# Column sums of the norms: folded on DVE and summed by one full product, in place of products with 32 columns of ones and a picking product

## Chip, cores and metric

One core of a Trainium2 chip runs the whole program. The metric is the device time of an execution in microseconds. TensorE is PE in the profile (PEld its weight loads), VectorE is DVE, ScalarE is ACT, GpSimd is POOL.

## What is computed

A sequence of 256 tokens with 1024 channels goes through two transformer stacks. The first has two layers (a state space branch and windowed attention, then a gated feed-forward part), the second four layers, each with another mixer (a conformer convolution, a gated linear recurrence, an mLSTM, stick-breaking attention) and a gated feed-forward part with a convolution. Everything is float32. What the change touches are the norms after each branch:

```python
def rms_norm(x, w):
    y = xf * lax.rsqrt(jnp.mean(xf * xf, axis=-1, keepdims=True) + NORM_EPS)
    return y * w
...
def layer_norm(x, g, b):
    mu = jnp.mean(xf, axis=-1, keepdims=True)
    var = jnp.mean(jnp.square(xf - mu), axis=-1, keepdims=True)
    y = (xf - mu) * lax.rsqrt(var + LN_EPS)
    return y * g + b
...
x = x + mixed @ w_out[i]                                  # first stack, then rms_norm
...
x = layer_norm(DN_ALPHA * x + (1.0 + gate1) * y, ...)     # second stack
```

## The kernel before, in words

The residual `x` lies in SBUF as 8 tiles of 128 channels (partitions) by 256 tokens. `h` is its normalised copy, the input of the next projections; `t1` (`sb_t` in the trace) holds squares. `L` are four PSUM banks for products of weights (`job_bank`), `M` four for the rest (`mix_bank`).

A **job** is a projection to two tiles of output channels. `run` computes one with products of 128x128 weights and 256 columns (L892). Weights come through a ring of five slots of 1 MB, filled by the SP queue (L664), in the order of use.

At the end of a branch (`w_out`, `w_down` and so on) four jobs give the 8 tiles of `x`. Around the norm the program is cut in halves of 128 tokens, so that the norm of one half runs beside products of the other. The last `ns` jobs (1 or 2) are computed as **half passes** (`half_pass`, L947): first tokens 0 to 127 of them, then tokens 128 to 255 into the banks M[2] and M[3]. Then `heads` computes the first two jobs of the next stage, first half of both (with the h of tokens 0 to 127), and then the second half. A half of a job is 16 products where the contraction has 8 tiles, 32 where it has 16 and 44 where it has 22. `hooks` puts other instructions behind the n-th product of a half pass.

A norm needs for each token the sum over 1024 channels of x squared, and in the "mean" norms (second stack) of x as well. The order of the work around it:

- For each job that is done in full, DVE updates x (`add_to_x` L2488, `gated_to_x` L2338) and ACT writes the squares of the two tiles to `t1` (`square_pair`, L1771). In the "mean" norms DVE adds up squares into t1[0:2] and values into t1[2:4] (`gather`, L2354 and L2356); in the "square" norms it makes one add, t1[0:2] += t1[4:6] (L2306).
- `pair_sums` (L980, last=True): four products of 32 columns of ones with t1[0..3], 256 tokens each, into the four row groups of M[0]. It stands behind the first half pass of the first tail job.
- For each half the tail job's tiles are updated (`add_tail` L2498, `gated_tail` L2378), squared by ACT, and summed by `tail_sums` with `group_sums` (L961): products with 32 columns of ones, in "square" one for each tile of squares, in "mean" also one for each tile of x.
- DVE copies M[0] to SBUF (`keep_parts`, L2300), and `whole_sums` adds the four groups and spreads the total over 128 partitions by a product with a picking matrix (`pick`): one in "square" (L1007), two in "mean" (L1001, L1002), into M[1].
- ACT takes the root (L1791, L1818), DVE the reciprocal (L2291, L2413), and DVE (L2294) or DVE and ACT (L2405, L2408, L1804) make h.

The first half's group stands in the second half pass of the tail (behind 8 products), the second half's in the first half pass of the heads (behind 8, or 12 with ns = 2), each with the picking products 2 ("mean") or 4 ("square") further on (`join_hooks`).

There are 11 such norms: four "square" with ns = 1 in the first stack; in the second stack four "mean" with ns = 1 (after the feed-forward parts of layers 0 to 2 and after the mLSTM) and three with ns = 2 (after `pw2` of the conformer, the recurrence and the stick-breaking attention). The last norm of the second stack (`final_norm`) and the norm within the conformer go their own ways, though the latter shares `whole_sums`, `keep_parts` and `centre_half`. In the feed-forward parts of the first stack and of layers 0 and 1 of the second, work for the conditioning of later layers goes along; there two transposes (L1102) stand between the tail's second half pass and the heads. Behind pw2 the order is written out by hand:

```python
half_pass(pw2[2], h_tile, 0).then_inc(s.half_done, 1)
half_pass(pw2[0], h_tile, 1, h_first)
half_pass(pw2[1], h_tile, 1)
pair_sums("mean")
half_pass(pw2[3], h_tile, 0).then_inc(s.half_done, 1)
pair_sums("mean", True)
half_pass(pw2[2], h_tile, 1, bank=M[2], hooks=join_hooks("mean", pw2, 2, 0))
```

So DVE gets jobs 0 and 1 of pw2 in full only just ahead of the tail, where the other norms get them earlier.

Of the kernel before, what the change touches and what calls it, by code (L numbers as in the profile page):

```python
# [366 lines left out]
def build(nc, a, out):  # L367
    with ExitStack() as ctx:
# [494 lines left out]
        def _(pe):  # L863
# [94 lines left out]
            def group_sums(norm, ks, c):  # L958

                def into(g, src):  # L960
                    return pe.matmul(M[0][32 * g:32 * g + 32, c], ones[:, 0:32], src, start=False, stop=True,  # L961
                                     skip_group_check=True)
                if norm == "mean":
                    for k in ks[::2]:
                        into(0, x[:, k, c])
                        into(1, x[:, k + 1, c])
                        into(2, t1[:, k, c])
                        mm = into(3, t1[:, k + 1, c])
                else:
                    for k in ks:  # L970
                        mm = into(k % 4, t1[:, k, c])
                return mm

            def pair_sums(norm, last=False):

                due(s.sq_ready)
                if last:
                    pe.wait_ge(s.acc_ready, due(s.acc_ready))
                    for g, k in enumerate((2, 3, 0, 1) if norm == "mean" else range(4)):
                        pe.matmul(M[0][32 * g:32 * g + 32, 0:T], ones[:, 0:32], t1[:, k, :], start=True, stop=True,  # L980
                                  skip_group_check=True)

            def tail_sums(norm, jobs_, ns, half):

                if half == 0:
                    read_out(pe, jobs_[-1])
                else:
                    pe.wait_ge(s.tail_x, due(s.tail_x))
                pe.wait_ge(s.sq_ready, due(s.sq_ready))
                group_sums(norm, range(KD - 2 * ns, KD), slice(half * P, (half + 1) * P))\  # L990
                    .then_inc(s.sum_ready, 1)

            def whole_sums(norm, half):

                c = slice(half * P, (half + 1) * P)
                pe.wait_ge(s.part_ready, due(s.part_ready))
                part = std[:, T + half * P:T + (half + 1) * P]
                if norm == "mean":
                    if half:
                        pe.wait_ge(s.var_ready, due(s.var_ready, 2) - 1)  # L1000
                    pe.matmul(M[1][:, c], pick[:, 0, :], part, start=(half == 0), stop=True, skip_group_check=True)  # L1001
                    mm = pe.matmul(M[1][:, T + half * P:T + (half + 1) * P], pick[:, 1, :], part, start=False, stop=True,  # L1002
                                   skip_group_check=True)
                else:
                    if half:
                        pe.wait_ge(s.std_ready, due(s.std_ready, 2) - 1)
                    mm = pe.matmul(M[1][:, c], pick[:, 2, :], part, start=(half == 0), stop=True, skip_group_check=True)  # L1007
                mm.then_inc(s.stat_ready, 1)

            def join_hooks(norm, jobs_, ns, half):  # L1010

                at = 8 if half == 0 or ns == 1 else 12
                gap = 2 if norm == "mean" else 4
                return {at: lambda: tail_sums(norm, jobs_, ns, half), at + gap: lambda: whole_sums(norm, half)}

            def project(jobs_, rhs, ready, norm, ns=1, hook=None):

                for i, job in enumerate(jobs_[:-ns]):
                    run(job, rhs, ready if i == 0 else None)
                    if hook:  # L1020
                        hook(i)
                    if i:
                        pair_sums(norm)
                project_tail(jobs_, rhs, norm, ns, hook)

            def project_tail(jobs_, rhs, norm, ns=1, hook=None):

                tail = jobs_[-ns:]
                for n, job in enumerate(tail):
                    half_pass(job, rhs, 0).then_inc(s.half_done, 1)  # L1030
                    if n == 0:
                        pair_sums(norm, True)
# [25 lines left out]
            def last_project(jobs_, rhs, ready):  # L1058
# [17 lines left out]
                pe.wait_ge(s.tail_x, due(s.tail_x))  # L1076
# [88 lines left out]
            for l in range(L1):  # L1165
# [197 lines left out]
                for i in range(1, 3):  # L1363
                    fill(mixed_part(i, 1))
                    pair_sums("square")
# [35 lines left out]
            lo, hi, whole = slice(0, P), slice(P, T), slice(0, T)  # L1401
            fill(depthwise(3, M[2], whole))
# [15 lines left out]
            whole_sums("mean", 0)  # L1418
# [7 lines left out]
            half_pass(pw2[0], h_tile, 0, h_first, hooks={8: last_sums, 12: lambda: whole_sums("mean", 1)})  # L1426
# [4 lines left out]
            pair_sums("mean")  # L1431
            half_pass(pw2[3], h_tile, 0).then_inc(s.half_done, 1)
            pair_sums("mean", True)
# [318 lines left out]
        def _(act):  # L1752
# [20 lines left out]
            def tail_squares(jobs_, ns, half):  # L1773

                if half == 0:
                    read_out(act, jobs_[-1])
                else:
                    act.wait_ge(s.tail_x, due(s.tail_x))
                square_pair(KD // 2 - ns, slice(half * P, (half + 1) * P), 2 * ns)

            def rms(jobs_, ns, modulate=None):
# [4 lines left out]
                for half in range(2):  # L1786
# [4 lines left out]
                    act.activation(std[:, c], M[1][:, c], ACT.Sqrt, scale=1.0 / D, bias=eps[:, 0:1])\  # L1791
# [476 lines left out]
        def _(vec):  # L2268
# [33 lines left out]

            def rms_tail(jobs_, ns, w, dst, signal):
# [991 lines left out]
```

## Time and profile before

| | |
|---|---|
| median of 3 runs | 2521.22 us (2521.11 to 2521.43) |
| the profiled execution, time | 2521.86 us |
| its span | 2520.0 us |
| PE busy | 2502.0 us (99%) |
| PEld busy | 2175.5 us (86%) |
| DVE busy | 1307.3 us (52%) |
| ACT busy | 550.4 us (22%) |
| POOL busy | 166.8 us (7%) |
| granted TensorE clock, mean | 0.999 of full speed |

The span is the time from the first to the last recorded instruction; the execution's own time is a little longer. A matrix product in float32 shows as two records of PE and two of PEld. Records of products overlap in time, so the starts of the weight loads show the pace of TensorE better than the busy time does.

### The profile page before, as it was taken

The page shows a single profiled execution, that of the slowest core. Times are in us where ns is not written, and L with a number is a line of the kernel's source. Part 1 is how long each engine was busy: PE and PEld are TensorE (multiplying, and loading weights), DVE is VectorE, ACT ScalarE, POOL GpSimd, SP SyncE. Part 2 cuts the span into 40 slices and gives each one's busy share as a digit, 9 for nine tenths or more (in the row PEclk, how much of TensorE's full clock was granted, in tenths as well). Part 3 has the DMA queues.
Part 4 walks back from the last instruction along what each step waited for, and adds up shares of the span by engine and source line. Part 5 has one row for each costly group of instructions (what it writes and reads, how often), then busy time and mean ns, then how long its engine had stood idle before and what let it go on. Part 6 is the DMA issues. An engine that isn't in the chain of part 4 may idle for free.

```text
span 2520.0 us, 35293 instructions
## 1 busy us (share of the span) xinstructions
PE 2502.0 (99%) x14764; PEld 2175.5 (86%) x14764; DVE 1307.3 (52%) x3091; ACT 550.4 (22%) x1081; POOL 166.8 (7%) x268
## 2 busy tenths in 40 slices
PE   9999999999999999999999999999999999999998
PEld 7879888987888898988898988898889889889888
DVE  6652774565278637498444479742534332324332
ACT  3451100144200022311041311023412111432101
POOL 2000110000031000011000121030000000000000
PEclk9999999999999999999999999999999999999999
DMA  7935885573389645588544488643244444334442
GB/s 217 225 98 192 288 290 199 144 193 102 120 295 317 234 147 148 201 305 291 171 153 132 140 301 296 231 147 99 86 146 139 151 156 145 117 117 152 152 157 76
DMA packets 403241, 457.96 MB, mean 182 GB/s; under 512 B 50751, under 2 KB 374776, under 8 KB 403084
## 3 DMA queue, kind: packets, MB, share of 16 engines
q1 hardware_dynamic: 370098, 340.53, 43.3%
q0 software_dynamic: 29936, 112.73, 12.5%
q10 hardware_dynamic: 3050, 2.46, 0.4%
q8 instruction: 117, 1.92, 0.3%
q14 instruction: 40, 0.33, 0.0%
HBM read 451.48 MB, written 1.29 MB: 180 GB/s over the span
## 4 chain that ended last, share of the span: by engine, by line
PE 96%; DVE 2%; ACT 0%; DMA 0%; issue 0%; SPq 0%; DVEq 0%; ACTq 0%
PE job_bank L892 68%; PE job_bank L947 11%; PE mix_bank L947 4%; PE job_bank L1317 3%; DVE sb_arena L2549 1%; PE mix_bank L1228 1%; PE mix_bank L1264 1%; PE job_bank L1292 1%; PE mix_bank L1565 1%; PE mix_bank L1278 1%; DVE sb_arena L2523 1%; PE mix_bank L923 1%; PE mix_bank L1609 0%; PE mix_bank L961 0%; PE mix_bank L1700 0%
## 5 line engine op out<-in xcount | busy, mean ns | idle before, releaser
L892 PE MATMUL job_bank<-sb_h,sb_ring 128*128 128x256 f32 (+1 forms) x5920 | 1300.3, 380 | 0.0
L892 PEld LDWEIGHTS job_bank<-sb_h,sb_ring 128*128 128x128 f32 (+1 forms) x5920 | 1115.2, 190 | 168.8 <-issue 17.1
L892 PE MATMUL job_bank<-sb_arena,sb_ring 128*128 128x256 f32 x1840 | 401.3, 380 | 0.0
L892 PEld LDWEIGHTS job_bank<-sb_arena,sb_ring 128*128 128x128 f32 x1840 | 348.6, 190 | 51.1 <-issue 3.5
L2523 DVE SCALAR_TENSOR_TENSOR sb_arena<-sb_arena,sb_par 128x256 f32<-128x256 f32 x722 | 333.9, 502 | 13.3
L2549 DVE SCALAR_TENSOR_TENSOR sb_arena<-sb_arena,sb_c_act 128x256 f32<-128x256 f32 x672 | 326.0, 485 | 24.0
L1767 ACT ACTIVATE sb_arena<-job_bank 128x512 f32<-128x512 f32 x178 | 106.2, 597 | 1025.8 <-PE job_bank L892 967.5
L947 PE MATMUL job_bank<-sb_h,sb_ring 128*128 128x128 f32 x1600 | 185.8, 276 | 1.4 <-ACT sb_h L2056 1.4
L947 PEld LDWEIGHTS job_bank<-sb_h,sb_ring 128*128 128x128 f32 x1600 | 181.5, 192 | 4.0 <-issue 3.0
L833 POOL DMA_DIRECT2D sb_arena<-in_ada_w x96 | 84.9, 885 | 850.6 <-DVE sb_arena L2549 533.2
L2521 DVE TENSOR_SCALAR sb_arena<-sb_arena,sb_par 128x256 f32<-128x256 f32 x263 | 97.0, 412 | 77.6 <-ACT sb_arena L1767 77.4
L2620 DVE TENSOR_TENSOR sb_arena<-sb_arena 128x512 f32<-128x512 f32 x44 | 30.6, 696 | 202.5 <-ACT sb_arena L1829 202.0
L2338 DVE SCALAR_TENSOR_TENSOR sb_x<-job_bank,sb_ada,sb_x 128x256 f32<-128x256 f32 x42 | 18.4, 480 | 221.5 <-PE job_bank L892 212.3
L1771 ACT ACTIVATE sb_t<-sb_x 128x512 f32<-128x512 f32 (+1 forms) x52 | 29.3, 564 | 472.3 <-DVE sb_x L2338 219.8
L947 PEld LDWEIGHTS mix_bank<-sb_arena,sb_ring 128*128 128x128 f32 x784 | 89.8, 192 | 5.1 <-issue 5.1
L947 PE MATMUL mix_bank<-sb_arena,sb_ring 128*128 128x128 f32 x784 | 94.0, 277 | 0.0
L1317 PE MATMUL job_bank<-sb_arena,sb_ring 128*128 128x256 f32 x384 | 90.3, 384 | 0.0
L947 PEld LDWEIGHTS job_bank<-sb_arena,sb_ring 128*128 128x128 f32 x784 | 89.1, 192 | 0.9 <-issue 0.4
L947 PE MATMUL job_bank<-sb_arena,sb_ring 128*128 128x128 f32 x784 | 89.4, 275 | 0.0
L1317 PEld LDWEIGHTS job_bank<-sb_arena,sb_ring 128*128 128x128 f32 x384 | 70.2, 190 | 14.6 <-issue 6.4
L892 PE MATMUL job_bank<-sb_ring,sb_h 128*128 128x256 f32 x320 | 73.4, 382 | 0.0
L2488 DVE TENSOR_TENSOR sb_x<-sb_x,job_bank 128x512 f32<-128x512 f32 x12 | 8.2, 687 | 123.9 <-PE job_bank L892 69.2
(452 smaller groups left out, 1729.1 us busy)
## 6 DMA issues: line engine op xcount, KB each, us to landing
sb_arena<-in_ada_w POOLq DMA_DIRECT2D x96, 1024.0 KB, 7.5
sb_ring<-in_ffn_w_up SPq DMA_DIRECT2D x88, 1024.0 KB, 5.1
sb_ring<-in_w_up SPq DMA_DIRECT2D x44, 1024.0 KB, 7.4
sb_ring<-in_ffn_w_down SPq DMA_DIRECT2D x32, 1024.0 KB, 5.2
sb_ring<-in_w_in SPq DMA_DIRECT2D x24, 1024.0 KB, 5.8
sb_ring<-in_w_down SPq DMA_DIRECT2D x16, 1024.0 KB, 6.9
sb_ring<-in_hg_w_in SPq DMA_DIRECT2D x16, 1024.0 KB, 5.5
sb_ring<-in_ml_w_up SPq DMA_DIRECT2D x16, 1024.0 KB, 5.5
```

What stands on the lines that cost most here:

```text
L833: pool.dma_start(ada_w[:, n % ADA_RING, :, :], src).then_inc(ada_in[n % ADA_RING], 16)
L892: mm = pe.matmul(o, st, mv, start=(k0 + k == 0 and t == 0), stop=(k0 + k == kn - 1), skip_group_check=True)
L923: mm = pe.matmul(M[3][32 * j:32 * j + 32, 0:UC], unit_sel[:, 31 - r:63 - r], ada_part[:, (first + j) % ADA_PARTS, :], start=(r == 0), stop ...
L947: mm = pe.matmul(o[:, t, c], w[:, k, t * P:(t + 1) * P], rhs(k0 + k)[:, c], start=(k0 + k == 0 and t == 0 and (half == 0 or bank is not No ...
L1228: mm = pe.matmul(bank[e * HD:(e + 1) * HD, c], xt[:, j, i * HD:(i + 1) * HD], g[:, e, :], start=(n == 0), stop=(n == 3), skip_group_check= ...
L1317: mm = pe.matmul(bank[:, t, :], slot(unit)[:, k, t * P:(t + 1) * P], mixed(u * KD + k), start=(u == 0 and k == 0 and t == 0), stop=(u == 1 ...
L1767: act.activation(dst, pair(L[job[0] % 4]), func).then_inc(bank_read[job[0] % 4], 1)
L1771: act.activation(t1[:, 2 * i:2 * i + n, c], x[:, 2 * i:2 * i + n, c], ACT.Square).then_inc(s.sq_ready, 1)
L2521: i = vec.tensor_scalar(o, ins_[0], ws[0], b, ALU.mult, ALU.add)
L2523: i = vec.scalar_tensor_tensor(out=o, in0=ins_[j], scalar=ws[j], in1=o, op0=ALU.mult, op1=ALU.add)
L2549: ins = vec.scalar_tensor_tensor(out=o, in0=w, scalar=c_act[:, k:k + 1], in1=o, op0=ALU.mult, op1=ALU.add)
L2620: vec.tensor_tensor(fact[:, 2 * i:2 * i + 2, :], fcv[:, i % 2, 0:2, :], fcv[:, i % 2, 2:4, :], ALU.mult).then_inc(s.act_ready, 1)
```

## The change

The four row groups, the picking matrix (at these norms) and `pair_sums` go. DVE folds everything to one tile of squares, t1[0], and two tiles of values, t1[2] and t1[3], for each half; TensorE then sums over the partitions with a full 128x128 square of ones, whose result stands on all partitions at once: one product for the squares, two more that accumulate for the values. Half 0 uses M[0], half 1 uses M[1]. The hooks are moved: squares behind 10 products in the first half, behind 7 + 4 ns in the second, the values two products before. ACT squares the tail pairs one by one in the first half.

```diff
-            def group_sums(norm, ks, c):
-            def pair_sums(norm, last=False):
-            def tail_sums(norm, jobs_, ns, half):
...
+            def x_sums(half):
+                c = slice(half * P, (half + 1) * P)
+                pe.wait_ge(s.acc_ready, due(s.acc_ready))
+                for k in (2, 3):
+                    pe.matmul(M[half][:, 0:P], ones[:, :], t1[:, k, c], start=(k == 2), stop=(k == 3),
+                              skip_group_check=True)
+            def square_sums(norm, half):
+                c = slice(half * P, (half + 1) * P)
+                at = P if norm == "mean" else 0
+                pe.wait_ge(s.acc_ready, due(s.acc_ready))
+                pe.matmul(M[half][:, at:at + P], ones[:, :], t1[:, 0, c], start=(norm != "mean"), stop=True,
+                          skip_group_check=True).then_inc(s.stat_ready, 1)
...
             def join_hooks(norm, jobs_, ns, half):
-                at = 8 if half == 0 or ns == 1 else 12
-                gap = 2 if norm == "mean" else 4
-                return {at: lambda: tail_sums(norm, jobs_, ns, half), at + gap: lambda: whole_sums(norm, half)}
+                at = 10 if half == 0 else 7 + 4 * ns
+                hooks = {at: lambda: square_sums(norm, half)}
                 if norm == "mean":
+                    hooks[at - 2] = lambda: x_sums(half)
+                return hooks
...
             def tail_squares(jobs_, ns, half):
-                if half == 0:
-                    read_out(act, jobs_[-1])
-                else:
+                c = slice(half * P, (half + 1) * P)
+                if half:
                     act.wait_ge(s.tail_x, due(s.tail_x))
-                square_pair(KD // 2 - ns, slice(half * P, (half + 1) * P), 2 * ns)
+                    square_pair(KD // 2 - ns, c, 2 * ns)
+                    return
+                for n, job in enumerate(jobs_[-ns:]):
+                    read_out(act, job)
+                    square_pair(KD // 2 - ns + n, c)
...
+            def add_x(i, c, last):
+                settle()
+                ins = vec.tensor_tensor(t1[:, 2:4, c], t1[:, 2:4, c], x[:, 2 * i:2 * i + 2, c], ALU.add)
...
+            def add_squares(i, c):
+                settle()
+                step(vec.tensor_tensor(t1[:, 0:2, c], t1[:, 0:2, c], t1[:, 2 * i:2 * i + 2, c], ALU.add))
+            def fold_squares(c):
+                settle()
+                vec.tensor_tensor(t1[:, 0, c], t1[:, 0, c], t1[:, 1, c], ALU.add).then_inc(s.acc_ready, 1)
             def rms_tail(jobs_, ns, w, dst, signal):
                 vec.wait_ge(s.sq_ready, due(s.sq_ready, KD // 2 - ns))
-                vec.tensor_tensor(t1[:, 0:2, :], t1[:, 0:2, :], t1[:, 4:6, :], ALU.add).then_inc(s.acc_ready, 1)
+                for i in range(1, KD // 2 - ns):
+                    add_squares(i, slice(0, T))
                 for half in range(2):
+                    c = slice(half * P, (half + 1) * P)
                     add_tail(jobs_, ns, half)
-                    due(s.sq_ready)
-                    keep_parts(half)
+                    if half:
+                        due(s.tail_x)
+                    vec.wait_ge(s.sq_ready, due(s.sq_ready))
+                    add_squares(KD // 2 - ns, c)
+                    fold_squares(c)
...
             def post_norm(jobs_, ns, n):
                 l, which = n // 2, n % 2
-                due(s.sq_ready, 2)
+                first = KD // 2 - ns
                 for half in range(2):
-                    gated_tail(jobs_, ns, half, l, which)
-                    centre_half(half, x)
+                    c = slice(half * P, (half + 1) * P)
+                    if half == 0:
+                        for m in range(ns):
+                            gated_tail(jobs_, ns, 0, l, which, (m,))
+                            read_out(vec, jobs_[m - ns])
+                            add_x(first + m, c, m == ns - 1)
+                            vec.wait_ge(s.sq_ready, due(s.sq_ready))
+                            add_squares(first + m, c)
+                    else:
+                        gated_tail(jobs_, ns, 1, l, which)
+                        vec.wait_ge(s.tail_x, due(s.tail_x))
+                        for m in range(ns):
+                            add_x(first + m, c, m == ns - 1)
+                        vec.wait_ge(s.sq_ready, due(s.sq_ready))
+                        for m in range(ns):
+                            add_squares(first + m, c)
+                    fold_squares(c)
+                    centre_half(half, x, M[half][:, 0:P], M[half][:, P:2 * P])
```

TensorE at the first norm of the first stack ("square"), before. L947 in `job_bank` with `sb_arena` is the first half of the tail, in `mix_bank` its second half, in `job_bank` with `sb_h` the heads:

```order
L947 MATMUL job_bank<-sb_arena,sb_ring 128x128 x32
L980 MATMUL mix_bank<-sb_t,sb_ones 32x256 x4
L947 MATMUL mix_bank<-sb_arena,sb_ring 128x128 x8
L961 MATMUL mix_bank<-sb_t,sb_ones 32x128 x2
L947 MATMUL mix_bank<-sb_arena,sb_ring 128x128 x4
L1007 MATMUL mix_bank<-sb_std,sb_pick 128x128
L947 MATMUL mix_bank<-sb_arena,sb_ring 128x128 x20
L947 MATMUL job_bank<-sb_h,sb_ring 128x128 x8
L961 MATMUL mix_bank<-sb_t,sb_ones 32x128 x2
L947 MATMUL job_bank<-sb_h,sb_ring 128x128 x4
L1007 MATMUL mix_bank<-sb_std,sb_pick 128x128
L947 MATMUL job_bank<-sb_h,sb_ring 128x128 x52
```

The same place now:

```order
L947 MATMUL job_bank<-sb_arena,sb_ring 128x128 x32
L947 MATMUL mix_bank<-sb_arena,sb_ring 128x128 x10
L971 MATMUL mix_bank<-sb_t,sb_ones 128x128
L947 MATMUL mix_bank<-sb_arena,sb_ring 128x128 x22
L947 MATMUL job_bank<-sb_h,sb_ring 128x128 x11
L971 MATMUL mix_bank<-sb_t,sb_ones 128x128
L947 MATMUL job_bank<-sb_h,sb_ring 128x128 x53
```

Ten small products became two full ones, and the hooks stand 10 and 11 products into their passes.

DVE at the norm behind pw2 ("mean", ns = 2), from the last full update of x (L2338) to the statistics of the first half, before:

```order
L2338 SCALAR_TENSOR_TENSOR sb_x<-job_bank,sb_ada,sb_x 128x256 x4
L2354 TENSOR_TENSOR sb_t<-sb_t 128x512
L2356 TENSOR_TENSOR sb_t<-sb_x 128x512
L2378 SCALAR_TENSOR_TENSOR sb_x<-job_bank,sb_ada,sb_x 128x128 x4
L2300 COPY sb_std<-mix_bank 128x128
L2393 TENSOR_SCALAR sb_red<-mix_bank 128x128
```

and now (L2374 is the tail's update, L2280 the value add, L2289 the square add, L2294 the fold):

```order
L2336 SCALAR_TENSOR_TENSOR sb_x<-job_bank,sb_ada,sb_x 128x256 x4
L2352 TENSOR_TENSOR sb_t<-sb_t 128x512
L2354 TENSOR_TENSOR sb_t<-sb_x 128x512
L2374 SCALAR_TENSOR_TENSOR sb_x<-job_bank,sb_ada,sb_x 128x128 x2
L2280 TENSOR_TENSOR sb_t<-sb_t,sb_x 128x2x128
L2289 TENSOR_TENSOR sb_t<-sb_t 128x2x128
L2374 SCALAR_TENSOR_TENSOR sb_x<-job_bank,sb_ada,sb_x 128x128 x2
L2280 TENSOR_TENSOR sb_t<-sb_t,sb_x 128x2x128
L2289 TENSOR_TENSOR sb_t<-sb_t 128x2x128
L2294 TENSOR_TENSOR sb_t<-sb_t 128x128
L2388 TENSOR_SCALAR sb_red<-mix_bank 128x128
```

The four updates of the tail no longer stand together: the adds of the first tail pair stand between them. The value product (L963) waits for the second L2280, the square product (L971) for L2294.

## Rows read from the trace of the kernel before

**Rows 1.** The page's busy line, and from the waits TensorE's at L947 and the DMA queue's
```profile
PE 2502.0 (99%) x14764; PEld 2175.5 (86%) x14764; DVE 1307.3 (52%) x3091; ACT 550.4 (22%) x1081; POOL 166.8 (7%) x268
...
PE job_bank L947 <- ACT sb_h L2056: 1.4, 1, 1.4
...
SPq L664 <- PE job_bank L892: 1734.8, 251, 17.9
```

**Rows 2.** Timeline of weight loads, first "square" norm: start, us, engine line op xcount
```profile
216.81 6.33 PEld L947 LDWEIGHTS job_bank<-sb_arena,sb_ring 128*128 128x128 f32 x56
...
223.83 1.86 PEld L947 LDWEIGHTS mix_bank<-sb_arena,sb_ring 128*128 128x128 f32 x16 [0.41 <-issue]
...
226.16 0.97 PEld L947 LDWEIGHTS mix_bank<-sb_arena,sb_ring 128*128 128x128 f32 x8 [0.20 <-issue]
...
227.27 4.55 PEld L947 LDWEIGHTS mix_bank<-sb_arena,sb_ring 128*128 128x128 f32 x40
...
235.18 11.69 PEld L947 LDWEIGHTS job_bank<-sb_h,sb_ring 128*128 128x128 f32 x104
```

**Rows 3.** Groups by form: all records of L980, L961 and L1001 (busy, mean ns, idle)
```profile
L961 PE MATMUL mix_bank<-sb_t,sb_ones 128*32 128x128 f32 x112 | 10.4, 282 | 0.0
...
L961 PE MATMUL mix_bank<-sb_x,sb_ones 128*32 128x128 f32 x80 | 7.1, 281 | 0.0
L980 PE MATMUL mix_bank<-sb_t,sb_ones 128*32 128x256 f32 x88 | 7.0, 391 | 0.0
...
L1001 PE MATMUL mix_bank<-sb_std,sb_pick 128*128 128x128 f32 x32 | 6.8, 294 | 0.0
```

**Rows 4.** Timeline of weight loads, first "mean" norm with ns = 1
```profile
1259.81 1.86 PEld L947 LDWEIGHTS mix_bank<-sb_arena,sb_ring 128*128 128x128 f32 x16 [0.41 <-issue]
1261.79 0.11 PEld L961 LDWEIGHTS mix_bank<-sb_x,sb_ones 128*32 128x32 f32 x2
1261.80 0.11 PEld L961 LDWEIGHTS mix_bank<-sb_t,sb_ones 128*32 128x32 f32 x2
...
1262.14 0.52 PEld L947 LDWEIGHTS mix_bank<-sb_arena,sb_ring 128*128 128x128 f32 x4 [0.20 <-issue]
...
1263.07 7.67 PEld L947 LDWEIGHTS mix_bank<-sb_arena,sb_ring 128*128 128x128 f32 x68
```

**Rows 5.** Timeline of weight loads, norm behind pw2, ns = 2
```profile
1025.32 1.86 PEld L947 LDWEIGHTS mix_bank<-sb_h,sb_ring 128*128 128x128 f32 x16 [0.41 <-issue]
...
1027.88 0.52 PEld L947 LDWEIGHTS mix_bank<-sb_h,sb_ring 128*128 128x128 f32 x4 [0.20 <-issue]
...
1028.81 4.99 PEld L947 LDWEIGHTS mix_bank<-sb_h,sb_ring 128*128 128x128 f32 x44
```

**Rows 6.** Groups by form on DVE: adds and updates of half and full width
```profile
L2408 DVE TENSOR_TENSOR sb_x<-sb_x,sb_rstd 128x256 f32<-128x256 f32 x28 | 10.9, 430 | 0.5
...
L2354 DVE TENSOR_TENSOR sb_t<-sb_t 128x512 f32<-128x512 f32 x11 | 7.6, 692 | 8.7 <-ACT sb_t L1771 8.7
...
L2397 DVE SCALAR_TENSOR_TENSOR sb_rstd<-mix_bank,sb_red 128x128 f32<-128x128 f32 x16 | 4.7, 292 | 0.5
```

**Rows 7.** Timeline of DVE and ACT, first half of the first "square" norm
```profile
223.37 0.42 DVE L2498 TENSOR_TENSOR sb_x<-sb_x,job_bank 128x256 f32<-128x256 f32 x1 [5.07 <-PE job_bank L947]
...
223.83 0.42 ACT L1771 ACTIVATE sb_t<-sb_x 128x256 f32<-128x256 f32 x1 [6.25 <-DVE sb_x L2498]
```

**Rows 8.** Timeline, second half of the norm behind the mLSTM, ns = 1
```profile
1902.34 1.87 PEld L947 LDWEIGHTS job_bank<-sb_h,sb_ring 128*128 128x128 f32 x16
...
1902.65 0.61 DVE L2378 SCALAR_TENSOR_TENSOR sb_x<-mix_bank,sb_ada,sb_x 128x128 f32<-128x128 f32 x2 [0.39 <-PE mix_bank L947]
...
1903.62 1.63 ACT L1804 ACTIVATE sb_h<-sb_x,sb_lnp 128x128 f32<-128x128 f32 x4
```

**Rows 9.** Timeline of weight loads and DVE ahead of the tail behind pw2
```profile
1016.85 7.79 PEld L947 LDWEIGHTS job_bank<-sb_h,sb_ring 128*128 128x128 f32 x69
...
1024.30 1.18 DVE L2378 SCALAR_TENSOR_TENSOR sb_x<-job_bank,sb_ada,sb_x 128x128 f32<-128x128 f32 x4
```

More of the change, by code:

```diff
@@ L974, in pair_sums @@
-            def pair_sums(norm, last=False):
-                due(s.sq_ready)
[L977 to L981, printed above, removed]
-            def tail_sums(norm, jobs_, ns, half):
-                if half == 0:
[L986 to L1008, printed above, removed]
@@ new lines, in square_sums, with whole_sums @@
+            def square_sums(norm, half):
[4 more added lines that the diff above has]
+                          skip_group_check=True).then_inc(s.stat_ready, 1)
+            def whole_sums(half):
+                c = slice(half * P, (half + 1) * P)
+                pe.wait_ge(s.part_ready, half + 1)
+                part = std[:, T + half * P:T + (half + 1) * P]
+                if half:
+                    pe.wait_ge(s.var_ready, 1)
+                pe.matmul(M[1][:, c], pick[:, 0, :], part, start=(half == 0), stop=True, skip_group_check=True)
+                pe.matmul(M[1][:, T + half * P:T + (half + 1) * P], pick[:, 1, :], part, start=False, stop=True,
+                          skip_group_check=True).then_inc(s.stat_ready, 1)
@@ L1417, in _ @@
             fill(rest, 4)
-            whole_sums("mean", 0)
+            whole_sums(0)
             fill(rest)
@@ L1424, in last_sums @@
                 norm_sums((5, 6, 7), hi).then_inc(s.sum_ready, 1)
-            half_pass(pw2[0], h_tile, 0, h_first, hooks={8: last_sums, 12: lambda: whole_sums("mean", 1)})
+            half_pass(pw2[0], h_tile, 0, h_first, hooks={8: last_sums, 12: lambda: whole_sums(1)})
             half_pass(pw2[1], h_tile, 0)
@@ L1790, in rms @@
                     act.wait_ge(s.stat_ready, due(s.stat_ready))
-                    act.activation(std[:, c], M[1][:, c], ACT.Sqrt, scale=1.0 / D, bias=eps[:, 0:1])\
+                    act.activation(std[:, c], M[half][:, 0:P], ACT.Sqrt, scale=1.0 / D, bias=eps[:, 0:1])\
                        .then_inc(s.std_ready, 1)
@@ L2344, in gated_to_x, with gather @@
                         step(ins)
-            def gather(job, i, last):
+            def gather(job, i):
                 n = due(s.sq_ready)
@@ L2368, in tail_done, with gated_tail @@
                     vec.wait_ge(s.unit_used, done_units(job))
-            def gated_tail(jobs_, ns, half, l, which):
+            def gated_tail(jobs_, ns, half, l, which, ms=None):
                 c = slice(half * P, (half + 1) * P)
                 for n, job in enumerate(jobs_[-ns:]):
+                    if ms is not None and n not in ms:
+                        continue
                     tail_done(job, half)
@@ L2635, in glu @@
                         if l < L2 - 1:
-                            gather(job, i, i == KD // 2 - 2)
+                            gather(job, i)
                 if stack == 1 and l == 0:
```

54 lines of the change are left out of this document (18 added, 36 removed).

## The prediction

> **What bounds the kernel now.** I read the busy shares first, then TensorE's waits, then the loads of its weights in the order of time. TensorE is busy 99% of a span of 2520.0 us, DVE half of it, and of all waits of TensorE only one, of 1.4 us, stands at the products of the half passes; the DMA queue spends its time waiting until TensorE frees a ring slot, so the weights are ahead [rows 1]. So TensorE's stream is the time: a product taken out of it is worth its own length, and a product that waits costs the wait. ACT and DVE matter only where a TensorE instruction waits for them, which at the norms is a question of tenths of a microsecond.
>
> A product in f32 is two records. In the long run of half pass products 104 loads take 11.69 us, the last of them 0.19: a pitch of (11.69 - 0.19) / 103 = 0.1117 us, or **0.223 us per product** of 128 by 128 with 128 columns [rows 2]. What a group of sum products costs is then the time from one pass row's first load to the next one's, less the pitches of the pass loads in it.
>
> **The change, part by part.** There are 11 norms with two halves each: four of kind "square" and seven of kind "mean" (four with ns = 1, three with ns = 2). The counts agree: 88 loads of L980 are 11 times 8, 192 loads of L961 are 4 x 8 + 4 x 16 + 3 x 32, and of the 32 loads of L1001 28 are the seven norms' and 4 the conformer's own, which stays [rows 3].
>
> Removed from TensorE. (1) The four products of `pair_sums` (256 columns): from 216.81 to 223.83 are 7.02 us with 56 pass loads, 6.26 us, so 0.77 each norm [rows 2]. (2) The column sums of L961 in a half: "square" 226.16 - 223.83 - 16 x 0.1117 = 0.54 [rows 2]; "mean" with ns = 1, four products, 0.55 [rows 4]; with ns = 2, eight products, 2.56 - 1.79 = 0.77 [rows 5]. (3) The picking products: one at "square", 227.27 - 226.16 - 8 x 0.1117 = 0.22 [rows 2]; two at "mean", 0.93 - 0.45 = 0.48 [rows 4, 5]. By norm: square 0.77 + 2 x (0.54 + 0.22) = 2.29; ns = 1 0.77 + 2 x (0.55 + 0.48) = 2.83; ns = 2 0.77 + 2 x (0.77 + 0.48) = 3.27. Together 4 x 2.29 + 4 x 2.83 + 3 x 3.27 = **30.3 us**.
>
> Added to TensorE. A half gets one full product for the squares, 0.223, and in "mean" two more for the values, which I price as the pair of picking products that they resemble (full array, 128 columns, a wait ahead), 0.48. That is 8 x 0.223 + 14 x (0.223 + 0.483) = **11.7 us**. The nearest rows bound this closely: no full product of 128 columns is shorter than two pitches, and the pairs with a wait cost 0.04 over four.
>
> The surprise of the rows is how dear the small products are. Four products of 32 columns stand over one another in time (their loads start 0.01 us apart in [rows 4]), and yet the group costs 0.55 us, since the array idles 0.20 us behind it and 0.41 us behind L980 with no releaser but issue [rows 2, 4]. The Trainium skill, "TensorE: Matmul & The Clock Gate", section "Measured speedup vs the span model", says the opposite of what this change needs: small tiles run concurrently, in the time of one product and about 4 ns per tile, so that a full square of ones gives away a speedup. The skill's "TensorEngine Tiling (Array Packing)", "Key Properties", says that a change of tiling mode drains the array; the idle 0.20 and 0.41 us agree with it. The sum goes by the measured group; the packing rule is a rival below.
>
> Added to DVE, with cover. "Square": one more full add after the third pair (0.69, as L2354), and in each half an add of 128x256 and one of 128x128 in place of the copy of L2300. "Mean": one add of values and one of squares for each tail pair and half, and the fold. Prices: 0.43 for 128x256 and 0.29 for 128x128 [rows 6]. That is about 6 us over the "square" norms and 17 over the "mean" ones on an engine that is half idle; what counts is whether the fold is done when TensorE comes to its product. Call S the start of the last load before a pass.
>
> - Square, first half: S = 223.83 - 0.77 - 0.11 = 222.95. DVE's tail add starts at 223.37, S + 0.42, and ACT's squares end 0.88 later, S + 1.30 [rows 7]. Then about 0.10 for the semaphore, 0.43, 0.03 and 0.29: S + 2.15, and some 0.07 to TensorE. The product stands behind ten others: S + 0.11 + 2.23 = S + 2.34. It fits, by 0.1 us. The second half stands behind eleven and has 0.3.
> - Mean, ns = 1: the tail updates start at S + 0.42 and end 0.61 later, the squares end at about S + 1.5, the two adds at S + 2.35; the product stands behind ten and two, S + 2.79. In the second half the pass comes to the fifth tile of h after eight products, S + 1.90, without the old group ahead of it; that tile is ACT's first after the squares, at 1903.62 + 0.48 = 1904.10, or S + 1.87 with S = 1902.34 - 0.11 [rows 8]. Zero to 0.1 us, in the two norms of this kind without transposes ahead of the heads: 0.1 in all.
> - Mean, ns = 2: with a half pass of job 2 ahead, the work of pair 2 is done under job 3's; the last pair has the timing of ns = 1. The exception is pw2. There the full jobs end late, and DVE comes to the tail only at 1024.30, while S = 1016.85 + 68 x 0.1117 = 1024.45 [rows 9]. Now DVE has to do pair 2 whole (updates 0.61, value add 0.45, a wait for ACT's squares, square add: 1.5 us, to 1025.8), then pair 3's updates and its value add, 1026.9; TensorE wants the values at S + 1.90 = 1026.35. A **new wait of 0.5 us**, once. The squares follow in time behind it.
>
> Behind a TensorE wait stand the pass products and all that follows; In a half the statistics are there about a microsecond earlier relative to S, as no group of L980 and no copy to DVE and back stands before them, and the pass ends about a microsecond sooner too, so the first tile of h keeps its distance to the heads. The loads of weights start when slots come free, in the same order, and the queue is ahead by hundreds of microseconds of waiting [rows 1]. ACT's split squares cost two starts, hidden.
>
> Sum: -30.3 + 11.7 + 0.5 + 0.1 = **-18.0 us**. The profiled execution took 2521.86 us (span 2520.0); the median of the runs is 2521.22. The forecast on the median is 2521.2 - 18.0 = **2503.2 us**, 0.7% faster. About 0.2% (5 us) is what a measurement of this kernel can tell from no change. The likeliest case's own range is 2501 to 2505.
>
> **The rivals.**
> *The chain of adds comes late.* The slack of 0.1 to 0.4 us rests on prices of the nearest operations. If each of the 22 halves waits 0.2 us, 4.4 us are given back: 2507.6. For: the fold product at "square" has only 0.1 us. Against: the halves of "mean" have 0.4 us and more. Chance 0.17.
> *The idle time belongs to the wait, not to the small tiles.* If the 0.20 us behind a group returns behind each of the 36 new groups that wait, 7.2 us come back: 2510.4. Against: the picking products also wait, and no idle time stands behind them [rows 2, 4, 5]. Chance 0.04.
> *The small tiles cost only their own streaming.* If what follows a group hid its idle time anyway, L980 was worth two products' time, 0.45, L961 one, 0.22 (two, 0.45, at ns = 2), and the removed work is 4 x 1.34 + 4 x 1.86 + 3 x 2.31 = 19.7 us, so the change gives 19.7 - 11.7 - 0.6 = 7.4: 2513.8. This is what the packing rule of the Trainium skill's page "TensorE: Matmul & The Clock Gate" would make of it. Against: groups are measured by what the stream loses, at every norm. Chance 0.03.
> *Slower.* TensorE stands at the fold products because DVE and ACT need more than a microsecond over my prices in each half. The point is 18.6 / 22 = 0.85 us of waiting in a half, and 1.1 for a loss of 5 us: 2526. It would take adds of half width at the price of full ones (0.69) with 0.3 us between steps. Against: [rows 6]. Chance 0.02.
> *The change does less than it says*, some of the removed groups coming back elsewhere: the order of instructions shows 69 fewer rows on TensorE and none of L961, L980 or L1007 left outside the conformer. The rest, 0.02, stands for this, at about 2516.
> The forecast keeps 0.72.
>
> **How the numbers follow.** 2501 to 2508 holds the forecast and most of the late chain, about 0.85, and leaves out the others. Faster by over 0.2% are all cases but the last two: 0.96; within 0.2% 0.02; slower 0.02.
>
> **What would show it.** TensorE still without waits of note, but one of about 0.5 us at the first value product after pw2; 30 us of L961, L980, L1001 and L1007 gone, 50 products with the full ones (100 records) instead, at 0.223 us each in the stream; no idle 0.20 or 0.41 us between pass loads at the joins; from 223.0 us a first pass of 32 + 1 products in 7.4 us where it took 8.7 with L980. Wrong would be: waits of TensorE for DVE in most halves (the first rival), idle time behind the new groups (the second), or a gain of half the size without waits (the third).

## The result, and the profile after

The changed kernel takes 2503.54 us (median of 5 runs, 2501.99 to 2504.18), the kernel before beside it 2521.11 us (5 runs, 2520.55 to 2521.43): a ratio of 0.9929, 95% interval 0.9918 to 0.9940. The profiled execution took 2504.18 us, its span is 2502.4 us, 17.6 us less than before. Two executions of the runs below took some thousand microseconds more (9749 us for the kernel before, 6709 us for the last variant), and no ratio counts them.

The page's busy line of the changed kernel, to be held against the one in [rows 1]:

```profile
PE 2483.4 (99%) x14512; PEld 2169.8 (87%) x14512; DVE 1330.2 (53%) x3143; ACT 551.4 (22%) x1084; POOL 167.3 (7%) x268
```

TensorE has 252 records fewer and is still busy 99% of the time; DVE has 22.9 us more. Three of TensorE's waits (engine, line, what it waited for: us, times, longest):

```profile
...
PE job_bank L947 <- ACT sb_h L2030: 1.4, 1, 1.4
PE mix_bank L1358 <- issue: 1.2, 1, 1.2
...
PE mix_bank L963 <- DVE sb_t L2280: 0.3, 1, 0.3
```

The first is the one that [rows 1] has too. Then there is one wait for DVE at a norm, as forecast, and one entry that was not: `issue` (no releaser that the profile shows) at L1358, a line of the conformer's convolution, which the change does not touch. More on it below.

The first square norm, timeline of weight loads, in place of [rows 2]:

```profile
223.06 2.31 PEld L947 LDWEIGHTS mix_bank<-sb_arena,sb_ring 128*128 128x128 f32 x20
225.29 0.30 PEld L971 LDWEIGHTS mix_bank<-sb_t,sb_ones 128*128 128x128 f32 x2
225.52 4.99 PEld L947 LDWEIGHTS mix_bank<-sb_arena,sb_ring 128*128 128x128 f32 x44
230.43 2.54 PEld L947 LDWEIGHTS job_bank<-sb_h,sb_ring 128*128 128x128 f32 x22
232.89 0.30 PEld L971 LDWEIGHTS mix_bank<-sb_t,sb_ones 128*128 128x128 f32 x2
```

The idle 0.41 and 0.20 us of before are gone. From 223.06 to 230.43 the pass takes 7.37 us for 33 products, 0.223 each. The sum product is in the stream like any other.

Behind pw2, first half, timeline of DVE and of the weight loads, in place of [rows 5, 9]:

```profile
1017.84 0.60 DVE L2374 SCALAR_TENSOR_TENSOR sb_x<-job_bank,sb_ada,sb_x 128x128 f32<-128x128 f32 x2
1018.10 1.87 PEld L947 LDWEIGHTS mix_bank<-sb_h,sb_ring 128*128 128x128 f32 x16
...
1018.47 0.43 DVE L2280 TENSOR_TENSOR sb_t<-sb_t,sb_x 128x256 f32<-128x256 f32 x1
1019.00 0.42 DVE L2289 TENSOR_TENSOR sb_t<-sb_t 128x256 f32<-128x256 f32 x1
1019.35 0.60 DVE L2374 SCALAR_TENSOR_TENSOR sb_x<-job_bank,sb_ada,sb_x 128x128 f32<-128x128 f32 x2
...
1019.98 0.42 DVE L2280 TENSOR_TENSOR sb_t<-sb_t,sb_x 128x256 f32<-128x256 f32 x1
...
1020.46 0.52 PEld L963 LDWEIGHTS mix_bank<-sb_t,sb_ones 128*128 128x128 f32 x4 [0.50 <-DVE sb_t L2280]
```

The second pair's updates start only at 1019.35, behind the adds of the first pair, and the value products' loads, due at 1019.9, start at 1020.46. The group costs 0.57 us more than its pitches; the view of waits shows 0.3, since it counts only gaps in the modelled busy time of products.

**A ledger of the sum products.** As in the prediction, a group costs the time from the last pass load ahead of it to the first one behind it, less one pitch of 0.1117 us. Taken over all groups at the 11 norms:

| group | before, each | after, each |
|---|---|---|
| L980, four products, 256 columns | 0.77 (11 times) | none |
| L961, two / four / eight products, 128 columns | 0.543 (8) / 0.557 (8) / 0.775 (6) | none |
| picking: one L1007 / two L1001, L1002 | 0.223 (8) / 0.483 (14) | none |
| values: two L963 | none | 0.446 (13), 1.02 (1, pw2) |
| squares: one L971 | none | 0.223 (22) |
| sum | 30.5 us | 11.7 us |

The ledger says 18.7 us less, the medians 17.6. It holds two savings: small tiles are gone (8 + 8 + 6 groups of L961 and 11 of L980), and so are whole products (the picking ones, and those that DVE's adds replace). The first two experiments tell them apart.

### The profile page after: what moved, and what is told of

Same layout as the page of the kernel before. It is cut to its first block, busy times and chain, and to the rows that moved or that the text cites. A ratio compares the mean times of both kernels' runs of the same rounds, so it can differ in the third digit from the quotient of the medians.

```text
span 2502.4 us, 34856 instructions
## 1 busy us (share of the span) xinstructions
PE 2483.4 (99%) x14512; PEld 2169.8 (87%) x14512; DVE 1330.2 (53%) x3143; ACT 551.4 (22%) x1084; POOL 167.3 (7%) x268
## 4 chain that ended last, share of the span: by engine, by line
PE 96%; DVE 2%; ACT 0%; issue 0%; ACTq 0%; DMA 0%; DVEq 0%; SPq 0%
PE job_bank L892 69%; PE job_bank L947 11%; PE mix_bank L947 4%; PE job_bank L1290 3%; DVE sb_arena L2560 1%; PE mix_bank L1201 1%; PE mix_bank L1237 1%; PE job_bank L1265 1%; PE mix_bank L1536 1%; PE mix_bank L1251 1%; DVE sb_arena L2534 1%; PE mix_bank L923 1%; PE mix_bank L1580 0%; PE mix_bank L1671 0%; PE mix_bank L1600 0%
## 5 line engine op out<-in xcount | busy, mean ns | idle before, releaser
L947 PE MATMUL job_bank<-sb_h,sb_ring 128*128 128x128 f32 x1600 | 184.1, 275 | 1.4 <-ACT sb_h L2030 1.4
L947 PEld LDWEIGHTS job_bank<-sb_h,sb_ring 128*128 128x128 f32 x1600 | 181.2, 192 | 1.8 <-issue 1.6
L947 PE MATMUL mix_bank<-sb_arena,sb_ring 128*128 128x128 f32 x784 | 91.6, 275 | 0.0
L947 PEld LDWEIGHTS mix_bank<-sb_arena,sb_ring 128*128 128x128 f32 x784 | 89.6, 192 | 0.0
L947 PEld LDWEIGHTS job_bank<-sb_arena,sb_ring 128*128 128x128 f32 x784 | 89.0, 192 | 0.5
L947 PE MATMUL job_bank<-sb_arena,sb_ring 128*128 128x128 f32 x784 | 89.2, 275 | 0.0
```

The lines of the kernel that those rows point to most:

```text
L947: mm = pe.matmul(o[:, t, c], w[:, k, t * P:(t + 1) * P], rhs(k0 + k)[:, c], start=(k0 + k == 0 and t == 0 and (half == 0 or bank is not No ...
```

## The experiments

All are variants of the changed kernel, except one, timed beside the kernel before on the same chip (2521.35 us in the first series, 2521.06 in the second, 2521.49 in the third). A table after the last one sets the times beside the ledger.

**Small tiles with nothing else changed.** This asks whether the narrow products are what cost the time. Each full product of ones becomes four of 32 columns with the same tile, in the same place.

```diff
                 for k in (2, 3):
-                    pe.matmul(M[half][:, 0:P], ones[:, :], t1[:, k, c], ...)
+                    for g in range(4):
+                        pe.matmul(M[half][32 * g:32 * g + 32, 0:P], ones[:, 0:32], t1[:, k, c], ...)
...
-                pe.matmul(M[half][:, at:at + P], ones[:, :], t1[:, 0, c], ...)
+                for g in range(4):
+                    mm = pe.matmul(M[half][32 * g:32 * g + 32, at:at + P], ones[:, 0:32], t1[:, 0, c], ...)
```

> The changed kernel, but each full product of ones is replaced by four products of 32 columns of ones with the same tile, one into each row group of the same bank; DVE, ACT, waits and hooks are those of the changed kernel. Theory (the gain comes from leaving small column tiles, which cost a fixed time at each change of tile width): a group of four with 128 columns costs 0.56 us as before instead of 0.22, a group of eight 0.77 instead of 0.45, so 22 x 0.34 + 14 x 0.32 = 12 us of the gain go: about 2515.5 us. Rival (four small tiles run in the time of one product, and the gain came from fewer products or from other things): the same time as the changed kernel, 2503.5 us.

Measured: 2514.69 us (7 runs, 2513.67 to 2515.34), ratio to before 0.9973 (0.9962 to 0.9984). Of the 17.6 us 11 are gone, and only the products of ones differ, four narrow ones for each full one. The other 6.7 us of the gain stay (7.0 by the ledger): they come from the products that are no longer there. Its weight loads at the first mean norm with ns = 1:

```profile
1252.94 1.87 PEld L947 LDWEIGHTS mix_bank<-sb_arena,sb_ring 128*128 128x128 f32 x16
1254.93 0.38 PEld L964 LDWEIGHTS mix_bank<-sb_t,sb_ones 128*32 128x32 f32 x16
1255.51 0.52 PEld L947 LDWEIGHTS mix_bank<-sb_arena,sb_ring 128*128 128x128 f32 x4 [0.20 <-issue]
```

The idle 0.20 us is back, and the group of eight costs 0.775 us in the ledger (by the rounded rows 2.57 from first load to first load, less 16 pitches) where two full products cost 0.446; the group of four costs 0.556 for 0.223. By the ledger 11.7 us are given back, for the 12 expected. The rival of the packing, which allowed no difference, falls.

**The old group put back, with constant data.** Four products as L980 had them, then eight (`range(8)`), then one full product with 128 columns of ones in the same place. The extra products read a constant tile and write columns of a bank that later products overwrite.

```diff
+            def spare():
+                for g in range(4):
+                    pe.matmul(M[1][32 * (g % 4):32 * (g % 4) + 32, 0:T], ones[:, 0:32], par[:, 0:T], ...)
...
                     half_pass(job, rhs, 0).then_inc(s.half_done, 1)
+                    if n == 0:
+                        spare()
```

> The changed kernel with four extra products of 32 columns of ones with a constant tile of 256 columns, where the old kernel had its four of L980 (11 places; the second half's bank, overwritten later). Theory: 0.77 us each, 8.5 in all, 2512.0 us. Rival (small tiles cost their streaming alone, as one product of 256 columns): 0.45 each, 4.9 in all, 2508.5 us. If the old group had cost something for its data or its wait, this constant group would cost less than 0.77.

> As the run with four extra products, but eight in a row. Theory (a fixed cost of about 0.33 us for the change of tile width there and back, and 0.44 for each four that stream over one another): 1.21 us each, 13.3 in all, 2516.8 us. Rival (each small product costs its share, 0.19): 1.54 each, 16.9 in all, 2520.5 us. Rival (streaming alone): 0.89 each, 9.8 in all, 2513.3 us.

> The changed kernel with one extra full product (128 columns of ones, 256 columns of a constant tile) at the same 11 places. Both theories: no change of tile width, 0.44 us each, 4.9 in all, 2508.5 us, and no idle time around it. If a product of another source or bank among the pass products cost time of its own, it would be more than 0.5 each.

Measured: with four 2511.0 us (ratio 0.9959, 0.9944 to 0.9974), with eight 2515.47 us (0.9978, 0.9968 to 0.9987), with the full product 2508.49 us (4 runs, 2506.33 to 2510.21; 0.9947, 0.9930 to 0.9963). Weight loads at the first square norm, with four, with eight and with the full product:

```profile
221.84 2.42 PEld L947 LDWEIGHTS job_bank<-sb_arena,sb_ring 128*128 128x128 f32 x21
224.38 0.16 PEld L961 LDWEIGHTS mix_bank<-sb_par,sb_ones 128*32 128x32 f32 x8
224.95 2.20 PEld L947 LDWEIGHTS mix_bank<-sb_arena,sb_ring 128*128 128x128 f32 x19 [0.41 <-issue]
```

```profile
221.83 1.20 PEld L947 LDWEIGHTS job_bank<-sb_arena,sb_ring 128*128 128x128 f32 x10
223.15 0.59 PEld L961 LDWEIGHTS mix_bank<-sb_par,sb_ones 128*32 128x32 f32 x16
224.15 2.31 PEld L947 LDWEIGHTS mix_bank<-sb_arena,sb_ring 128*128 128x128 f32 x20 [0.41 <-issue]
```

```profile
221.91 1.87 PEld L947 LDWEIGHTS job_bank<-sb_arena,sb_ring 128*128 128x128 f32 x16
223.70 0.30 PEld L960 LDWEIGHTS mix_bank<-sb_par,sb_ones 128*128 128x128 f32 x2
224.03 2.42 PEld L947 LDWEIGHTS mix_bank<-sb_arena,sb_ring 128*128 128x128 f32 x20
```

Four cost 0.770 us and eight 1.201, at each of the 11 places. The full product costs 0.433: the first load behind it starts 0.329 us late, and the second one 0.104 more, which the ledger's rule leaves out. (No small group has such a second delay.) The second four cost 0.43, the time of that full product, so the four of a set do stream over one another; what is left, **0.34 us, is paid once per group**. With 128 columns it comes out the same: 0.557 for four and 0.775 for eight give 0.22 per four and again 0.34 once. The group with constant data costs what L980 cost, so neither its data nor a wait was in the price. By the times the full product brought 4.95 us over the changed kernel's median, 0.45 per place, but those runs lie up to 3.9 us apart, so the trace is the better source. (The full product also took up three quarters of the wait behind pw2, and the groups of small products all of it, so with them the times rise by some 0.5 us less than the price of the products.)

What the Trainium skill's page "TensorE: Matmul & The Clock Gate", section "Measured speedup vs the span model", says of small tiles thus holds for what it speaks of, the second four. Even here the small tiles are the cheaper way to sum four tiles as they are: 0.557 us for a group of four, 0.89 for four full products of 0.223. They lost to the full square since each group pays its 0.34 us, and since DVE's adds leave one tile to sum where there were several. The skill's "TensorEngine Tiling (Array Packing)", section "Key Properties", says that a change of the tiling mode drains the array; the 0.34 us once per group, with idle time behind it, agree.

**How much slack the adds have.**

```diff
-                at = 10 if half == 0 else 7 + 4 * ns
+                at = 7 if half == 0 else 4 + 4 * ns
```

> The changed kernel with all sum products three products (0.67 us) earlier in their passes. If the slack that the trace of the changed kernel shows is right (from the end of the DVE add plus 0.05 us: 0.21 us for the squares in the first half of the square norms, 0.44 and 0.66 in their second halves, 0.36 for the values in the first half of the mean norms, 0.59 and more in their second halves), TensorE waits 4 x 0.46, 2 x 0.23, 6 x 0.31, 2 x 0.08 us and 0.67 more behind pw2: 5.0 us in all, 2508.5 us. Rival (the products wait for something else, or an early product is made good later since the statistics come sooner): no loss, 2503.5 us.

Measured: 2508.4 us (ratio 0.9950, 0.9936 to 0.9963), 4.75 us over the changed kernel in the same series. TensorE's waits and the loads at the first square norm:

```profile
PE mix_bank L963 <- DVE sb_t L2280: 1.0, 1, 1.0
PE mix_bank L971 <- DVE sb_t L2294: 0.7, 4, 0.2
```

```profile
223.51 1.64 PEld L947 LDWEIGHTS mix_bank<-sb_arena,sb_ring 128*128 128x128 f32 x14
225.53 0.30 PEld L971 LDWEIGHTS mix_bank<-sb_t,sb_ones 128*128 128x128 f32 x2 [0.38 <-DVE sb_t L2294]
```

By the ledger the groups grew from 11.73 to 16.71 us, 4.98 for the 5.0 expected. The view of waits sees less of it (1.7 us), as at pw2; the loads show it whole. The chain of adds is thus what the sum products wait for, and nothing is made good later: the hooks in the changed kernel stand where they cost nothing, but for pw2, with 0.21 us in the tightest case.

**The place behind pw2.**

```diff
-            half_pass(pw2[2], h_tile, 1, bank=M[2], hooks=join_hooks("mean", pw2, 2, 0))
+            half_pass(pw2[2], h_tile, 1, bank=M[2], hooks={11: lambda: x_sums(0), 12: lambda: square_sums("mean", 0)})
```

> The changed kernel with the products behind pw2, first half, three and two products later (behind 11 and 12 in place of 8 and 10). Theory: the wait of 0.57 us of the first value product goes and nothing takes its place, 0.6 us less, 2503.0 us; too little for the times, to be read in the trace. Rival (the later statistics delay h or the second half's updates of x on DVE): a wait of the heads' products for h instead.

Measured: 2504.17 us (ratio 0.9932, 0.9917 to 0.9947), no difference to the changed kernel (2503.65 in this series) that the times could tell. In the trace the wait is gone: the group costs 0.446 us there as everywhere, the ledger is 11.16 us, and no wait for h took its place.

**The values folded to one tile too.** The longer chain of adds gets its hooks one product later in the first half of the mean norms (values behind 9, squares behind 11); behind pw2 they stand behind 13 and 15 in the first version, behind 11 and 12 in the second.

```diff
                 if last:
+                    settle()
+                    vec.tensor_tensor(t1[:, 2, c], t1[:, 2, c], t1[:, 3, c], ALU.add).then_inc(s.acc_ready, 1)
...
-                for k in (2, 3):
-                    pe.matmul(M[half][:, 0:P], ones[:, :], t1[:, k, c], start=(k == 2), stop=(k == 3), ...)
+                pe.matmul(M[half][:, 0:P], ones[:, :], t1[:, 2, c], start=True, stop=True, ...)
```

> The changed kernel with the values folded to one tile on DVE as well, so that each half of a mean norm has one value product, not two: 14 products of 0.223 us less, 3.1 us. DVE gets 14 more adds of 128x128 (0.33 us each with their step). The hooks are set to where the adds should be done: first half behind 9 and 11, behind pw2 behind 13 and 15. Theory: no new wait, the one behind pw2 gone: 2503.5 - 3.1 - 0.6 = 2499.8 us. Rival (the longer chain makes TensorE wait): up to 0.3 us in each of 14 halves comes back, 2504 us.

> As the run that folds the values to one tile, but the first half behind pw2 keeps its two value tiles, with products behind 11 and 12. There the longer chain had delayed DVE's update of the second half, ACT's squares and so the sixth tile of h, for which TensorE waited 0.85 us. Theory: that wait goes, one product of 0.22 us comes back, 0.6 us less than 2500.85: about 2500.2 us, no wait of TensorE at a norm. Rival: the delay comes from the fold of the second half, and the wait stays.

Measured: 2500.85 us (5 runs, ratio 0.9921, 0.9909 to 0.9934), and with the first half behind pw2 left at two tiles 2500.09 us (median of 4 runs, 2499.27 to 2503.28; ratio 0.9916, 0.9903 to 0.9930). In the first of the two the ledger fell to 8.03 us, but a wait came up in the second half behind pw2, here in its weight loads:

```profile
1026.23 1.12 DVE L2373 SCALAR_TENSOR_TENSOR sb_x<-mix_bank,sb_ada,sb_x 128x128 f32<-128x128 f32 x4
1027.38 0.63 ACT L1742 ACTIVATE sb_t<-sb_x 128x512 f32<-128x512 f32 x1 [0.54 <-DVE sb_x L2373]
...
1027.92 1.25 ACT L1778 ACTIVATE sb_h<-sb_x,sb_lnp 128x128 f32<-128x128 f32 x3
...
1028.45 0.74 PEld L947 LDWEIGHTS job_bank<-sb_h,sb_ring 128*128 128x128 f32 x6 [0.85 <-ACT sb_h L1778]
```

The later statistics of the first half kept DVE from the second half's updates, ACT squared later, and the sixth tile of h, which ACT makes behind those squares, came 0.85 us late: a wait two engines and one half away from its cause. In the second version, which changes the first half alone, no wait of TensorE at any of these norms is left and the ledger is 8.27 us. So the delay came from the first half and not from the second half's own fold; whether its add or its later hooks did more was not taken apart. Both are faster than the changed kernel by some 3 us, and between the two the times cannot tell. It is the best version of the study, 0.84% under the kernel before.

**Both kernels once more,** for the gap of 1.1 us between ledger and medians.

> The changed kernel once more, word for word. Its first trace has an idle time of 1.44 us of TensorE inside the conformer's convolution, where the kernel before had none, with no releaser but issue. Theory (the place follows from where the instruction stream is fetched, so from the kernel's layout): the same idle time at the same place, about 1.4 us. Rival (it comes and goes from run to run): another place or length, and the times of the runs scatter by it. The norms: the same 0.223 and 0.446 us per group, one wait of 0.57 us behind pw2. 2502 to 2504.5 us.

> The kernel before once more, word for word, to see whether the idle times of TensorE with no releaser (issue) in the conformer's convolution and at the state space scores belong to the changed kernel. Its first trace had 0.86 us at the norm sums there and none at the scores; the two traces of the changed kernel had 2.4 and 2.6 us above the pitch in the convolution, the second 1.4 more at the scores. Theory (they come and go with the run, in every kernel): another amount than in its first trace, and times of 2520 to 2522 us. Rival (the change brought them): the same amounts as in its first trace.

Measured: the changed kernel 2503.65 us (4 runs, 2502.84 to 2506.13; ratio 0.9933, 0.9919 to 0.9946), the kernel before 2521.44 us (10 runs, 2520.59 to 2522.22). The convolution's loads, in the changed kernel's first trace, in its second, and in the run with early hooks, which has the same instructions there:

```profile
986.89 0.22 PEld L1358 LDWEIGHTS mix_bank<-sb_arena 128*32 128x32 f32 x2
988.55 0.80 PEld L1358 LDWEIGHTS mix_bank<-sb_arena 128*32 128x32 f32 x29 [1.44 <-issue]
```

```profile
988.49 0.22 PEld L1358 LDWEIGHTS mix_bank<-sb_arena 128*32 128x32 f32 x2
990.44 0.80 PEld L1358 LDWEIGHTS mix_bank<-sb_arena 128*32 128x32 f32 x29 [1.73 <-issue]
```

```profile
988.81 0.89 PEld L1358 LDWEIGHTS mix_bank<-sb_arena 128*32 128x32 f32 x31
```

The idle time came back at the same load, with 1.44 and 1.73 us; in the third run it is not there. From the convolution's first product to the first one of pw2 the stage took 23.7 and 23.9 us in the changed kernel, 22.8 and 21.5 in the two traces of the kernel before, 21.3 with early hooks, 21.6 with the small tiles and with the group of four, 22.1 with the group of eight and with pw2 later, 23.8 with the full product, 23.6 and 22.7 with the two folds. So neither expectation holds alone: the length varies from trace to trace of one kernel, and with two traces of each it is not shown whether it also leans with the kernel. The new norms alone do not bring it, since the small tiles and the early hooks have them too. In the first pair of traces the stage makes up 0.9 of the 1.1 us.

| kernel (difference to the kernel before) | by the ledger, us | by the medians, us |
|---|---|---|
| changed, first and second time | -18.7 | -17.6, -17.4 |
| small tiles | -7.0 | -6.7 |
| group of 4 / of 8 added | -10.8 / -6.1 | -10.4 / -5.9 |
| full product added (at 0.433) | -14.4 | -12.9 |
| hooks early | -13.8 | -12.7 |
| pw2 later | -19.3 | -16.9 |
| values folded (with its wait for h) | -21.5 | -20.2 |
| values folded, but pw2 | -22.2 | -21.4 |

The order is that of the medians but for pw2 later, whose gain of 0.6 us is within their scatter. The rest is 0.2 to 0.5 us with the kernels that have small tiles at the norms and 0.8 to 2.4 with the others. In the second trace of the changed kernel TensorE also waited 0.9 us for DVE at the state space scores, and 1.1 us with pw2 later, where the rest is largest; in the changed kernel's first trace it did not. That too comes and goes.

## Why the prediction was right

The time, 2503.54 for a forecast of 2503.2, inside the likeliest case's own range, and its terms:

- *Removed, 30.3 us:* 30.5 in the ledger of all groups. It rested on reading the loads' starts and not the busy times: the products of L980 are busy 7.0 us in [rows 3], where the stream lost 8.5 with them, since the idle time behind a group stands in no busy row. The 33 small groups pay 33 times 0.34, 11.2 us, for standing among full ones; the rest is streaming and picking. That the idle time belongs to the small tiles was argued from the picking products, which wait and have none; the run with small tiles and those with constant groups show it.
- *Added, 11.7 us with pw2's 0.5 and 0.1 apart:* 11.73 with everything in. The pair of value products was over-sized, 0.48 for 0.446 (14 times, 0.5 us): the price came from the pair of picking products. The wait behind pw2 was 0.57 for 0.5, by the chain that was laid out. The 0.1 us for the fifth tile of h did not show.
- *DVE's chain:* priced at 0.43 and 0.29 for its adds, measured 0.428 and 0.296 (groups by form below); 23 us more on DVE, as forecast. The slack of the tightest case is 0.21 us, not 0.1, since DVE starts 0.03 us after ACT's squares end and not 0.10, and a product's loads 0.05 us after the add ends and not 0.07.

```profile
L2289 DVE TENSOR_TENSOR sb_t<-sb_t 128x256 f32<-128x256 f32 x28 | 12.0, 428 | 4.5 <-ACT sb_t L1742 3.9
...
L2294 DVE TENSOR_TENSOR sb_t<-sb_t 128x128 f32<-128x128 f32 x22 | 6.5, 296 | 0.8
```

- *The rivals:* the late chain fell (slack in all halves but one, and there the wait that was forecast), idle time that belongs to the wait fell (groups of 0.223 and 0.446 us exactly), packing fell. The slower side needed 0.85 us of waiting per half; there is none in 21 of 22.
- *What was missed:* the ledger alone gives 18.7 us and would have put the kernel at 2502.4. The forecast counted nothing for idle time outside the norms, and there some 1.1 us of the gain did not arrive. That the forecast came within 0.3 us of the median owes as much to its over-sized value products and its 0.1 us for h as to the sum; they stood in for a cost that it did not know.

What stays open is the cause of that idle time. It has no releaser, and it stands in a stretch of very short products (31 loads in 0.89 us). In six traces (both of the changed kernel, pw2 later, the two folds, and, eight loads ahead, the full product) it ends 1.2 to 1.5 us after a packet of 16 KB of the instruction queue has landed; with early hooks the packet landed 1.3 us ahead of the same load, and nothing idled. That points to the reading of the instruction stream. Against it stands the kernel before: its first trace idled at an earlier load, until 1.0 us after such a packet, and its second passed the same load 0.6 us before its packet landed and did not idle. No run changed that alone.

## What to carry to other kernels

Price a small product by what the stream around it loses, from the first load ahead of it to the first behind it, and not by its busy time: here four products of 32 columns streamed in the time of one and still cost two and a half times as much, because they stood alone among full ones. That is less than four full products, so the narrow ones should go only where the tiles can be added up first. If a reduction over partitions is needed in many places, let an engine with spare time fold first and hand TensorE one full square of ones, and set the product as many products late as the chain of adds is long; the slack can be read from the end of the last add to the start of the load. When a hook is moved later, follow the statistics on to the next half: what waits may be a tile of another engine there.

## What the runs showed of the hardware that was not expected

- A group of products of 32 columns among full ones costs the same 0.34 us beyond its streaming for four and for eight products, and for tiles of 128 and of 256 columns.
- A group of full products between other full products cost nothing but its pitches, 0.223 and 0.446 us, though it waits for another engine's semaphore and reads another tile, where the other engine ended in time; where it did not, the load started 0.05 us after the add's end.
- The convolution's stage took 21.3 to 23.9 us in the 12 traces, with the same 512 weight loads of the convolution and the same sums between them, and the executions of one version lie 0.3 us (group of four) to 4.0 us (the last variant) apart.
